# ScalarE and VectorE take gate function and tokens before the next expert's weights

## The reference

```python
scores = sigmoid(h @ w_router)                 # 64 experts, 8 are kept per token, from 4 of 8 groups
y_block = (silu(xb @ w_eg[e]) * (xb @ w_eu[e])) @ w_ed[e]     # 128 slots, one expert: 1024 -> 256 -> 1024
routed = zeros.at[row_tok].add(y_block * row_w)
out = routed + (silu(h @ w_sg) * (h @ w_su)) @ w_sd
```

## Time and profile before

| | |
|---|---|
| three runs | 3450.21, 3455.66, 3458.8 us, median 3455.66 |
| profiled execution | 3455.1 us, span 3453.3 us |
| TensorE busy | 3139.9 us, 91% |
| VectorE busy | 1740.1 us, 50% |
| ScalarE busy | 1369.1 us, 40% |
| GpSimd busy | 709.5 us, 21% |
| expert loop, first layer | from 1070 to 1909 us, 76 blocks |
| expert loop, second layer | from 2693 to 3410 us, 65 blocks |

### The profile page before, as it was taken

How to read it: one execution, slowest core, us unless ns; L and a number is a source line. 1 busy time by engine, 2 the same in 40 slices (tenths; PEclk the granted TensorE clock), 3 DMA queues, 4 the chain that set the end, 5 groups by cost and what they waited for, 6 DMA issues and landing times.

```text
span 3453.3 us, 49036 instructions
## 1 busy us (share of the span) xinstructions
PE 3139.9 (91%) x14864; PEld 2221.4 (64%) x14864; DVE 1740.1 (50%) x2560; ACT 1369.1 (40%) x1977; POOL 709.5 (21%) x767
## 2 busy tenths in 40 slices
PE   6999999999997999999999499999996899999994
PEld 3468877899545666666666346776863666666663
DVE  1354371222354666666666336362333666666665
ACT  2253251221224555555554235252212555555552
POOL 0000310000062333323332200020003332333332
PEclk9999999999999999999999799999998899999997
DMA  6420113333328999999998510113232999999993
GB/s 225 120 86 7 52 44 104 128 128 134 138 67 323 343 355 343 348 351 354 351 345 278 167 50 1 34 56 92 92 118 98 338 345 334 338 343 336 326 329 129
DMA packets 223714, 703.54 MB, mean 204 GB/s; under 512 B 55650, under 2 KB 104196, under 8 KB 169428
## 3 DMA queue, kind: packets, MB, share of 16 engines
q1 hardware_dynamic: 176356, 601.80, 47.0%
q0 software_dynamic: 47248, 100.21, 10.9%
HBM read 669.89 MB, written 98.31 MB: 222 GB/s over the span
## 4 chain that ended last, share of the span: by engine, by line
PE 63%; DMA 19%; DVE 6%; issue 6%; ACT 3%; SPq 2%; another core or an unknown queue 1%; DVEq 1%; POOLq 0%; POOL 0%; ACTq 0%
DMA ring<-in_w_exp_up 9%; PE ps L825 7%; PE ps L906 6%; PE ps L832 6%; PE ps L833 6%; PE ps L834 6%; DMA region_v<-in_w_exp_up 5%; PE ps L854 5%; PE ps L1104 4%; PE ps L877 4%; DMA region_k<-in_w_exp_up 4%; PE ps L879 4%; PE ps L878 4%; PE ps L1009 3%; PE ps L1030 3%
## 5 line engine op out<-in xcount | busy, mean ns | idle before, releaser
L1956 POOL DMA_INDIRECT acc<-region_q,idx_out x141 | 226.3, 1605 | 922.3 <-DVE region_q L1569 815.3
L877 PE MATMUL ps<-region_h_split,region_q_split 128*128 128x512 f32 x846 | 349.8, 413 | 69.1 <-DVE region_q_split L1529 33.7
L1535 DVE TENSOR_TENSOR ring_split<-ring,region_h_split 128x1024 fp32r<-128x1024 f32 x210 | 246.8, 1222 | 252.5 <-ACT region_h_split L1171 242.4
L854 PEld LDWEIGHTS ps<-con,region_c 128*128 128x128 f32 x1686 | 220.2, 167 | 147.1 <-DVE region_c L1542 73.6
L1171 ACT ACTIVATE region_h_split<-ring 128x1024 fp32r<-128x1024 f32 x210 | 210.1, 1052 | 240.8 <-DMA ring<-in_w_exp_up 201.3
L834 PE MATMUL ps<-region_x_split,ring_split 128*128 128x384 f32 (+2 forms) x800 | 283.0, 354 | 0.0
L854 PE MATMUL ps<-con,region_c 128*128 128x128 f32 x1686 | 258.0, 281 | 26.2 <-DVE region_c L1542 18.0
L906 PE MATMUL ps<-ring,region_c 128*128 128x512 f32 x560 | 252.0, 593 | 1.0 <-DVE region_c L1547 1.0
L1171 ACT ACTIVATE region_q<-ps 128x512 f32<-128x512 f32 (+1 forms) x163 | 106.8, 655 | 351.2 <-PE ps L906 233.9
L877 PEld LDWEIGHTS ps<-region_h_split,region_q_split 128*128 128x128 f32 x846 | 162.0, 192 | 117.6 <-issue 88.0
L878 PE MATMUL ps<-ring_split,region_q_split 128*128 128x512 f32 x560 | 219.9, 393 | 0.0
(11 more groups left out here) (315 smaller groups left out, 6909.9 us busy)
## 6 DMA issues: line engine op xcount, KB each, us to landing
ring<-in_w_exp_gate SPq DMA_DIRECT2D x70, 1024.0 KB
ring<-in_w_exp_up SPq DMA_DIRECT2D x70, 1024.0 KB
ring<-in_w_exp_down SPq DMA_DIRECT2D x70, 1024.0 KB
ring<-in_w_mod SPq DMA_DIRECT2D x24, 2048.0 KB, 8.0
region_k<-in_w_exp_gate SPq DMA_DIRECT2D x36, 1024.0 KB
region_k<-in_w_exp_up SPq DMA_DIRECT2D x36, 1024.0 KB
region_k<-in_w_exp_down SPq DMA_DIRECT2D x36, 1024.0 KB
region_v<-in_w_exp_gate SPq DMA_DIRECT2D x35, 1024.0 KB
```

The lines of the kernel that those rows point to most:

```text
L854: last = nc.tensor.transpose(ps[0:t.shape[1], at:at + t.shape[0]], t, ident[0:t.shape[0], 0:t.shape[0]])
L877: mm(m_gu[s], xT_hi[s][:, k, :], high, start=k == 0, stop=False)
L1535: tt(wgu_lo[w][:, :, 2 * c:2 * c + 2, :], wgu[w][:, :, 2 * c:2 * c + 2, :], wgu_hi[c], ALU.subtract).then_inc(sl["w_lo"], 1)
L1956: pool.indirect_dma_start(ACC[s], bass.IndirectOffsetOnAxis(ap=idx_out[:, s:s + 1], axis=0), yb[:, s, :], None, bounds_check=TOK - 1, oob_ ...
```

## The change

In the loop's turn, and in the first turn that stands ahead of the loop, `weights_of` moves on both engines from the first place to the place behind `tokens`. Its `If` is the one of `tokens`. Nothing else is changed: the same instructions, waits and buffers, on TensorE, GpSimd and SyncE the same order.

```diff
@@ scalar
                 act.sem_inc(sl["y_a"], 1)
                 tokens(0, 1)
-                weights_of(1, 1, 0)
                 silu(0, 1)
                 tokens(1, 2)
+                weights_of(1, 1, 0)
...
-                            with act.If(n + 1 < n_blocks):
-                                weights_of((r + 2) % UNROLL, m + (r + 2) // UNROLL + 1, n)
                             with act.If(n < n_blocks):
                                 silu(s, n + 1)
                             with act.If(n + 1 < n_blocks):
                                 tokens(1 - s, n + 2)
+                                weights_of((r + 2) % UNROLL, m + (r + 2) // UNROLL + 1, n)
                             with act.If(n <= n_blocks):
                                 act.wait_ge(sl["dn_done"], n)
@@ vector
                 weights_of(0, 0)
                 tokens(0, 1)
-                weights_of(1, 1)
                 hidden(0, 0, 0)
                 tokens(1, 2)
+                weights_of(1, 1)
                 turned_hidden(0, 0)
...
-                            with dve.If(n + 1 < n_blocks):
-                                weights_of((r + 2) % UNROLL, n + 1)
                             with dve.If(n < n_blocks):
                                 hidden(s, (r + 1) % UNROLL, n)
                             with dve.If(n + 1 < n_blocks):
                                 tokens(1 - s, n + 2)
+                                weights_of((r + 2) % UNROLL, n + 1)
                             with dve.If(n <= n_blocks):
                                 dve.wait_ge(sl["dn_done"], n)
```

## The result

The changed kernel takes 3434.88 us (median of 5 runs, 3433.47 to 3440.57) against 3455.55 us (5 runs, 3450.21 to 3458.8): a ratio of 0.9945, 95% interval 0.993 to 0.9959, or 20.7 us less. Forecast were 3445.5 us, 10 us less. The profiled execution took 3434.55 us with a span of 3432.8 us.

What follows compares the result with a forecast made beforehand. The busier half of the DMA engines was taken to set the pace in the expert loops. Only the loop ends gain: 3455.1 - 5.1 - 4.8 = 3445.2 us, put at 3445.5 against the runs' median, range 3425 to 3460.

Steps and rivals of the forecast that it cites:

- The path from landing to `gate_up`: Expert loops, from weights' arrival to TensorE's start: one VectorE piece left to wait for, 7.49 us down to 2.35 us.
- The unhindered turn: Expert-loop turn that no transfer holds: 10.0 us before, 10.2 us after, 0.15 us dearer.
- The ends: End of each expert loop, no more loads: shorter path paid once, 5.1 us in first layer, 4.8 us in second.
- In the middle of the loops: nothing: Mid-loop turns: slots asked for 5.1 us earlier, queue as much longer (about 29.6 us), turn length unchanged.
- the busier half: Expert loops: 8 of 16 DMA engines never stop and set the pace; the others idle 1.3 us a turn.
- The first rival, fuller DMA engines: Both loops: earlier requests fill idle DMA time, 49 us, with the ends 59 us, 3396 us at the utmost; chance 0.16.
- Results, additions and gathers some 3 us later in a turn: Expert loops: result copies, GpSimd's adding and gather come some 3 us later, covered because their users come a turn later.
- The clock: Rival, TensorE ahead of `gate_up`: one longer wait lowers its clock, 3484 us; chance 0.12, shared with a costly hand-over.
- The range and the chances: Whole kernel: range 3425 to 3460 us; faster 0.43, same 0.42, slower 0.15.
- the forecast's own one: Whole kernel: the forecast's own range, 3439 to 3452 us, given a chance of 0.56.
- The mechanism that was forecast: Ends of both expert loops: shorter path from landing to `gate_up` paid out once each, 5.1 and 4.8 us.

Runs made afterwards that it cites:

- after_early: Changed kernel with gate and up weights asked for as soon as `gate_up` is done, about 6 us earlier in a turn: 3438.53 us, ratio 0.9941.
- after_late: Changed kernel with gate and up weights asked for only when the block's down projection is done, 10 us later: 3467.58 us, ratio 1.003.
- before_early: Kernel before, order of pieces unchanged, with gate and up weights asked for as soon as `gate_up` is done: 3442.61 us, ratio 0.9952.
- dve_only: Half of the change: VectorE in the new order, ScalarE in its old one: 3450.45 us, ratio 0.9984 to the kernel before.
- short_placed: Changed kernel without the product of tokens' high part and weights' low part, rows spread over all DMA engines: 3293.85 us, ratio 0.9541.

## Why the prediction was right, and where it was wrong

- **The path from landing to `gate_up`, 7.49 to 2.35 us:** right. 2.37 us at 1404, at 1877 and at 3348.
- **The unhindered turn, 10.2 us:** nearly. TensorE takes 10.13 us in the many turns at the start of both loops that nothing holds, 0.1 us more than the 10.03 of before.
- **The ends, 5.1 and 4.8 us:** right, 10 us in sum as the traces split it, and 9 to 10 us in after_early and after_late too. One reading in it was wrong: 1876.82 in the earlier trace rows is not the landing of the last but one block's weights, since ScalarE was held by TensorE there (`<-PE ps L879`); they may have been there earlier. The split above therefore starts one block earlier.
- **"In the middle of the loops: nothing":** this is the step that failed. The way through the queue grew as forecast, from 24.6 to 28.8 us, but the landings then came 9 us sooner, and the turns shrank by 0.10 and 0.16 us. The reason given, that the pace is that of the busier half and a longer queue can't relieve it, was half right. The busier half is real: spreading the rows took 106 us away, and the dips to half a share are still there in the changed kernel (0.55 at 2961 and at 2992). But a queue that still holds 24.5 us of work when the next block is asked for was taken for one that can give nothing more, and before_early shows 12 to 15 us for 5 us more of it. How much of the 9 us is depth and how much the later additions and gathers stays open. The first rival, fuller DMA engines, had the right sign and was sized too high at half of its 49 us: 9 us.
- **Results, additions and gathers some 3 us later in a turn:** 3.8 us by the turns shown above. TensorE doesn't wait for the result, as said: between 2785 and 3350 all its waits over 0.1 us are for VectorE's pieces. What the shift does among the transfers was not thought of.
- **The clock:** the rival didn't come. Behind the single longer wait no slow stretch stands from 1165 to 1870 and from 2785 to 3350. That the four of before are gone is no clear gain of the change: they vary between executions, and dve_only has four.
- **The range and the chances:** 3434.88 us lies in the range and outside the forecast's own one (3439 to 3452). Faster was the likeliest sign. The mechanism that was forecast accounts for half of the 20.7 us; that the total still fell into the range is owed to its width.

## What to carry to other kernels

When a loop waits for a transfer, count what stands between its landing and the first instruction that needs it, and let everything that doesn't depend on it go first; that path is paid at the end of the loop, and in its middle it is worth what the requests that go out sooner bring. A mean DMA share below one beside a full queue can mean that the engines have unequal loads: look at 1 us windows for a level such as one half, and at which partitions the gathered rows lie on. Spreading them was worth five times the change of order, and left it without effect.

## What the runs showed of the hardware that was not expected

- With the same bytes, the 16 DMA engines carried 378 GB/s over 635 us where they had carried 348, by the partitions of the gathered and added rows alone, and about 381 to 386 GB/s in short_placed.
- The part between the loops differs by some 6 us among kernels that do the same there; the cause is open. From the last `gate_up` of the first loop to the first of the second it took 794.2 to 795.9 us in all four profiles with VectorE's old order, and 786.7 to 789.6 us in five of six with the new one (795.7 in the sixth), and 786.0 to 794.9 us in the four kernels without the third product. In the kernel before, a VectorE copy whose input TensorE had written 13 us earlier stands in the timeline as

```profile
2655.40 0.15 DVE L1813 COPY endc<-ps 64x1 f32<-64x1 f32 x1 [13.29 <-remote]
```

and in the changed kernel it waited 0.46 us, with 7.09 us before a later one. Nothing of the program is named as what the former waited for. In the changed kernel this part is 5.4 us shorter and the part ahead of the first loop 3.8 us longer, so that the whole span outside the loops is only 1.4 us shorter.
